# Feed-forward input products by Strassen's scheme, by token, in a two-layer trunk on one core

## What is computed

```python
def swiglu(h, w_in, w_out):                 # h: 512 x 1024, w_in: 1024 x 5632, w_out: 2816 x 1024
    gate, up = jnp.split(h @ w_in, 2, axis=-1)
    return (jax.nn.silu(gate) * up) @ w_out
x = x + 0.5 * swiglu(rmsnorm(x, norm_ffn1[layer]), w_ffn1_in[layer], w_ffn1_out[layer])
```

## Time and profile before

| | us |
|---|---|
| Median of three runs | 2101.12 |
| The profiled execution's own time | 2099.39 |
| Its span, first to last instruction | 2097.6 |
| TensorE busy | 2049.8 |
| VectorE busy | 960.4 |
| ScalarE busy | 592.3 |
| GpSimd busy | 244.6 |
| Granted TensorE clock, mean | 0.99 of full speed |

### The profile page before, as it was taken

One profiled execution on the slowest core, in us unless ns is written; L12 is line 12 of the kernel. 1 busy time (PEld: TensorE's weight loads), 2 busy tenths in 40 slices (PEclk: granted clock), 3 DMA queues, 4 the chain that ended last, 5 costly groups with the idle time before them and its releaser, 6 DMA issues.

```text
span 2097.6 us, 23288 instructions
## 1 busy us (share of the span) xinstructions
PE 2049.8 (98%) x9138; PEld 1674.5 (80%) x9138; DVE 960.4 (46%) x1173; ACT 592.3 (28%) x705; POOL 244.6 (12%) x155
## 2 busy tenths in 40 slices
PE   7999999999999999999999999999988899999997
PEld 5888888777877887888888788888867688888886
DVE  5444434433533444444444444443459754444333
ACT  4222222232222222222222222222256523222210
POOL 3000022110010141000022000002212050000021
PEclk9999999999999999999999999999989999999998
DMA  4222223222212222222223222223221022222221
GB/s 176 100 100 86 77 98 101 102 77 91 80 66 101 81 100 81 100 100 100 69 97 115 89 91 100 100 76 100 91 91 41 21 81 83 97 100 94 83 97 68
DMA packets 30962, 188.73 MB, mean 90 GB/s; under 512 B 3584, under 2 KB 3584, under 8 KB 14656
## 3 DMA queue, kind: packets, MB, share of 16 engines
q1 hardware_dynamic: 30672, 187.25, 25.6%
q0 software_dynamic: 240, 0.79, 0.1%
HBM read 185.92 MB, written 2.10 MB: 90 GB/s over the span
## 4 chain that ended last, share of the span: by engine, by line
PE 94%; DVE 3%; issue 1%; ACT 1%; DMA 0%; POOL 0%; POOLq 0%; DVEq 0%; SPq 0%; ACTq 0%
PE bank L1131 28%; PE bank L1133 28%; PE bank L1132 28%; PE bank L1137 2%; PE bank L1138 2%; PE bank L1139 2%; PE bank L1260 2%; DVE xn_lo L748 1%; PE bank L1250 1%; PE bank L1377 1%; PE bank L1366 1%; DVE w_lo L742 0%; PE bank L1414 0%; PE bank L1423 0%; DVE temp L1080 0%
## 5 line engine op out<-in xcount | busy, mean ns | idle before, releaser
L1131 PE MATMUL bank<-xn_hi,w_hi 128*128 128x512 f32 x1672 | 658.9, 394 | 16.5 <-DVE xn_lo L748 16.3
L1133 PE MATMUL bank<-xn_hi,w_lo 128*128 128x512 f32 x1672 | 652.4, 390 | 0.0
L1132 PE MATMUL bank<-xn_lo,w_hi 128*128 128x512 f32 x1672 | 652.3, 390 | 0.0
L480 ACT ACTIVATE w_hi<-w_raw 128x2048 fp32r<-128x2048 f32 (+2 forms) x195 | 335.7, 1722 | 1011.5 <-PE bank L1133 964.6
L742 DVE TENSOR_TENSOR w_lo<-w_raw,w_hi 128x2048 fp32r<-128x2048 f32 (+2 forms) x191 | 406.1, 2126 | 278.1 <-ACT w_hi L480 277.9
L1131 PEld LDWEIGHTS bank<-xn_hi,w_hi 128*128 128x128 f32 x1672 | 314.2, 188 | 88.9 <-DVE xn_lo L748 12.6
L1133 PEld LDWEIGHTS bank<-xn_hi,w_lo 128*128 128x128 f32 x1672 | 314.4, 188 | 66.8
L1132 PEld LDWEIGHTS bank<-xn_lo,w_hi 128*128 128x128 f32 x1672 | 314.5, 188 | 66.6 <-issue 2.2
L1131 PE MATMUL bank<-gated_hi,w_hi 128*128 128x512 f32 x704 | 273.9, 389 | 0.0
L1132 PE MATMUL bank<-gated_lo,w_hi 128*128 128x512 f32 x704 | 273.9, 389 | 0.0
L1133 PE MATMUL bank<-gated_hi,w_lo 128*128 128x512 f32 x704 | 273.9, 389 | 0.0
(11 more groups left out here) (154 smaller groups left out, 1588.4 us busy)
## 6 DMA issues: line engine op xcount, KB each, us to landing
w_raw<-w_ffn_in SPq DMA_DIRECT2D x87, 1024.0 KB, 4.7
w_raw<-w_ffn_out SPq DMA_DIRECT2D x64, 704.0 KB, 4.0
w_raw<-w_ret_in SPq DMA_DIRECT2D x24, 1024.0 KB, 4.8
w_raw<-w_ret_out SPq DMA_DIRECT2D x8, 1024.0 KB, 4.7
w_raw<-w_dsa SPq DMA_DIRECT2D x8, 1024.0 KB, 4.8
x_res<-x_in SPq DMA_DIRECT2D x4, 512.0 KB, 6.8
out<-x_res SPq DMA_DIRECT2D x8, 256.0 KB, 2.0
w_raw<-w_ffn_in SPq DMA_DIRECT2D x2, 512.0 KB, 6.8
```

The costliest lines, as they stand in the source:

```text
L480: nc.scalar.activation(w_hi[u % 2][:, :size], w_raw[u % 2][:, :size], copy)\
L1131: mm(to, w_hi[slot][:, at:at + width], hi, start=start, stop=False)
L1132: mm(to, w_hi[slot][:, at:at + width], lo, start=False, stop=False)
L1133: return mm(to, w_lo[slot][:, at:at + width], hi, start=False, stop=stop)
```

## The change

The input phase is done over for 20 of the 22 tiles, in five groups of four. With x in quarters (x11: features 0 to 511 of tokens 0 to 255, x12: the other features, x21 and x22 the same of tokens 256 to 511) and the weights of four tiles in quarters (w11 and w21 gate, w12 and w22 up; 512 columns each), a group's eight half-size products become seven (Winograd's form), each of 2 blocks of tokens x 4 feature chunks x 3 matmuls of 512 columns, by token. Four sums S1 to S4 of x quarters are made once in a sublayer, four sums T1 to T4 of weight quarters in every group, in place, all on VectorE. A weight quarter or sum is split in two parts of 1024 elements; four part slots (16 KB with hi and lo) are the ring between the splits and TensorE. The seven products are combined from PSUM on VectorE. The gated tiles come out token-major, so TensorE transposes them (fp32, by the identity, 16 of 128x128 a group) and ScalarE stores them. Tiles 20 and 21 (`REST`) are done plainly, by token, ahead of the groups, in four parts.

Beyond that: 1/rms is a per-token scalar, so the broadcast matmul of an ffn goes; the hi and lo of gated tiles are made at the end of the input phase (the hi copies lie where the weights were); the first two output chunks are done together, tile by tile, in `GATED_ORDER`; output weights have four slots; buffers of the ffn, retention and attention stages overlap, so first loads there wait for `unit_done`; rotary and decay tables load at the start of retention; x and weights are loaded in 1 KB rows (`load_rest`) and 2 KB rows (`load_quad`) in place of 8 KB rows; GpSimd's sums wait for the last transposes; loops of the ffn are written out.

Core of the diff (TensorE first, then VectorE, ScalarE):

```diff
+PRODUCTS = ("x11w11", "S1T1", "S2T2", "x12w21", "S3T3", "S4w22", "x22T4")
+GATED_ORDER = [8, 9, 10, 0, 1, 2, 3, 4, 5, 6, 7, 11, 12, 13, 14, 15, 20, 21, 16, 17, 18, 19]
+        def product_of_parts(to, hi, lo, slot, kk, start, stop):
+            part = slice(kk * P, (kk + 1) * P)
+            mm(to, hi, in_four(part_hi[slot])[:, :, part], start=start, stop=False)
+            mm(to, hi, in_four(part_lo[slot])[:, :, part], start=False, stop=False)
+            return mm(to, lo, in_four(part_hi[slot])[:, :, part], start=False, stop=stop)
...
+                for h in range(REST_PARTS):
+                    pe.wait_ge(part_lo_made, parts0 + h + 1)
+                    for kk in range(2):
+                        k = 2 * h + kk
+                        pe.wait_ge(xn_lo_made, CHUNKS * s + k + 1)
+                        for t in range(BLOCKS):
+                            done = product_of_parts(bank[(6, 7, 2, 3)[t]][:, :], tile(xn_hi, k * BLOCKS + t),
+                                                    tile(xn_lo, k * BLOCKS + t), part_slot(h), kk,
+                                                    k == 0, k == CHUNKS - 1)
+                    done.then_inc(part_used, 1)
+                    if h == (3 if s == 0 else 1):
+                        sum_over_features(norm)
...
+                def group_product(g, i):
+                    name = PRODUCTS[i]
+                    to = {"x11w11": 0, "x12w21": 0, "S2T2": 2, "S3T3": 2, "x22T4": 2, "S1T1": 4, "S4w22": 4}[name]
+                    for half in range(2):
+                        h = part_of(g, i, half)
+                        pe.wait_ge(part_lo_made, parts0 + h + 1)
+                        for kk in range(2):
+                            k = 2 * half + kk
+                            for t in range(2):
+                                hi, lo = left(name, k, t)
+                                done = product_of_parts(bank[to + t][:, :], hi, lo, part_slot(h), kk,
+                                                        k == 0, k == HALF_CHUNKS - 1)
+                        done.then_inc(part_used, 1)
+                def turn(g, half):
+                    from_, made = ((v, gated1_made), (p5, gated2_made))[half]
+                    pe.wait_ge(made, 2 * (GROUPS * f + g + 1))
+                    for n in range(2):
+                        pe.wait_ge(gated_stored, TURNED * f + 4 * g + 2 * half + n + 1)
+                        for m in range(2):
+                            for t in range(2):
+                                done = nc.tensor.transpose(tile(bank[6 + n], 2 * m + t),
+                                                           tile(from_[t], 2 * n + m), identity[:, :])
+                        done.then_inc(gated_turned, 1)
+                for g in range(GROUPS):
+                    count = 2 * (GROUPS * f + g)
+                    if g == 0:
+                        pe.wait_ge(mean_done, stat_count(norm))
+                    else:
+                        pe.wait_ge(gate1_summed, count)
+                    group_product(g, 0)
+                    if g == 0:
+                        turn_rest()
+                    else:
+                        turn(g - 1, 0)
+                    if g > 0:
+                        pe.wait_ge(up1_made, count)
+                    group_product(g, 1)
+                    if g > 0:
+                        turn(g - 1, 1)
+                        pe.wait_ge(gate2_summed, count)
+                    group_product(g, 2)
+                    pe.wait_ge(p1_copied, count + 2)
+                    group_product(g, 3)
+                    pe.wait_ge(u2_made, count + 2)
+                    group_product(g, 4)
+                    pe.wait_ge(p5_copied, count + 2)
+                    group_product(g, 5)
+                    pe.wait_ge(u3_made, count + 2)
+                    group_product(g, 6)
...
+                turn(GROUPS - 1, 0)
+                for half in range(2):
+                    for i in range(HALF_TILES * half, HALF_TILES * (half + 1)):
+                        pe.wait_ge(gated_lo_made, tile0 + i + 1)
+                        for d in range(2):
+                            done = out_product(d, 2 * half + d, i, i == 0, i == FF_TILES - 1)
+                        if i == 3:
+                            turn(GROUPS - 1, 1)
```

```diff
+                make_s1()
+                make_s2()
+                if s > 0:
+                    rest(s, 2)
+                    rest(s, 3)
+                mean_square(("norm", s), D_MODEL)
+                sum_lo(0)
+                make_s4()
+                sum_lo(1)
+                product_lo(0, 0)
+                add_quads(0, 0, 1, 0)
+                dve.wait_ge(r_col_done, stat_count(("norm", s)))
+                for g in range(GROUPS):
+                    end = g == GROUPS - 1
+                    if g == 0:
+                        rest_gated_tiles()
+                        product_lo(g, 1)
+                        sum_lo(3)
+                        make_s3()
+                    else:
+                        sum_gate_2(g - 1)
+                        product_lo(g, 1)
+                        gated_1(g - 1)
+                    add_quads(g, 0, 2, 1)
+                    if g > 0:
+                        gated_2(g - 1)
+                    product_lo(g, 2)
+                    if g == 0:
+                        s3_lo()
+                    add_quads(g, 1, 2, None, 0)
+                    product_lo(g, 3)
+                    make_u2(g)
+                    product_lo(g, 4)
+                    if end:
+                        split_unit(u0)
+                    make_v(g)
+                    add_quads(g, 3, 0, 3, 1)
+                    product_lo(g, 5)
+                    sum_gate_1(g)
+                    make_u3(g)
+                    up_2(g)
+                    product_lo(g, 6)
+                    up_1(g)
+                    if not end:
+                        product_lo(g + 1, 0)
+                        add_quads(g + 1, 0, 1, 0)
+                split_unit(u0 + 1)
+                gated_1(GROUPS - 1)
+                gated_lo_of(slice(0, 3))
+                sum_gate_2(GROUPS - 1)
+                gated_lo_of(slice(3, 5))
+                gated_2(GROUPS - 1)
+                gated_lo_of(slice(5, 11))
```

```diff
+        def split_part(f, h, source, ready=None):
+            if h >= REST_PARTS:
+                act.wait_ge(part_used, PARTS * f + part_before(h) + 1)
+            if ready is not None:
+                act.wait_ge(*ready)
+            nc.scalar.activation(in_four(part_hi[part_slot(h)]), source, copy).then_inc(part_hi_made, 1)
...
+                    product_hi(g, 1)
+                    if g > 0:
+                        gate_2(g - 1)
+                        store_turned(g - 1, 0)
+                    product_hi(g, 2)
+                    copy_product(g, 0, p1, p1_copied)
+                    if g > 0:
+                        store_turned(g - 1, 1)
+                    product_hi(g, 3)
+                    copy_product(g, 1, p5, p5_copied)
+                    product_hi(g, 4)
+                    product_hi(g, 5)
+                    product_hi(g, 6)
+                    gate_1(g)
+                    if not end:
+                        product_hi(g + 1, 0)
```

More of the change, by code:

```diff
@@ L85, in broadcast_count @@
 def broadcast_count(which):
[L87 to L88 removed]
+    return len([w for w in STATS[:stat_count(which)]
+                if w[0] == "head" or w[1] == len(SUBLAYERS) or SUBLAYERS[w[1]] == "ret"])
 def square_ops(which):
@@ new lines, in w_space_free, with part_slot, part_of, part_before @@
+    def w_space_free(engine, u):
+        s = stage_of(u)
+        n = u - FIRST_UNIT[s]
+        if SUBLAYERS[s] != "ffn" and n < 2:
+            engine.wait_ge(unit_done, FIRST_UNIT[s] - 1)
+    def part_slot(h):
+        return (2, 3, 0, 1)[h] if h < REST_PARTS else (h - REST_PARTS) % 4
+    def part_of(g, i, half):
+        return REST_PARTS + 2 * (N_PRODUCTS * g + i) + half
+    def part_before(h):
+        return max(m for m in range(h) if part_slot(m) == part_slot(h))
+    def parts_through(f, g, i):
+        return PARTS * f + part_of(g, i, 1) + 1
@@ new lines, in quad_half, with rest_part, in_four, stat_bank @@
+    def quad_half(n, half):
+        return quad[n][:, :].rearrange("p (t c) -> p t c", t=4)[:, :, 2 * P * half:2 * P * (half + 1)]
+    def rest_part(s, h):
+        return rest_raw[s][:, :].rearrange("p (t c) -> p t c", t=4)[:, :, 2 * P * h:2 * P * (h + 1)]
+    def in_four(t):
+        return t[:, :].rearrange("p (t c) -> p t c", t=4)
+    def stat_bank(which):
+        name, n = which
+        return 0 if name == "norm" and n < len(SUBLAYERS) and SUBLAYERS[n] == "ffn" else STAT_BANK
+    def rest_of(t):
+        return cols(rest_gated, t, 2 * P).rearrange("p (n c) -> p n c", n=2)
@@ L538, in _ @@
-                in_pair(FFN_IN_UNITS // 2 - 1, 0)
-                def out_tile(first, i):
-                    for n in range(2):
```

(45 more changed lines are left out.)

831 lines of the change are left out of this document (589 added, 242 removed).

## The result

The changed kernel takes 2046.33 us (2045.07 to 2047.51) against 2101.69 (2099.67 to 2104.12) of the kernel before, measured beside it: ratio 0.9736, with an interval from 0.9719 to 0.9753. That is 55 us less. The forecast was 2035, in a range of 2022 to 2080. The profiled execution's own time is 2046.45, its span 2044.7.

What follows compares the result with a forecast made beforehand. TensorE, busy 98% of the span, was taken as the bound. Phase savings of 73.5 us, less 3.2, 3.0 and 2.4, plus 1.3, gave 66.2: 2099.4 becomes 2033.2, stated as 2035 us, range 2022 to 2080.

Steps and rivals of the forecast that it cites:

- the floor: Input phase: 212.2 us of matmuls, 9.9 of turns and 0.8 of norm sums make at least 222.9 us.
- The 3.2 us of stalls: Groups: 0.2 us of TensorE stall at each of 16 tight places like gated_1 ahead of the turn.
- The first rival: Groups: VectorE paces them, its operations costing full durations; 24 to 32 us more, 2063; chance 0.24.
- 0.93 us a turn for 0.9: Input phases: each turn of 8 transposes costs TensorE 0.9 us, bounded at 0.8 and 1.2; 11 turns per sublayer.
- The stand-still of 5.4 us: First ffn, after the plain tiles: TensorE idles 5.4 us while VectorE waits for sum_over_features ahead of the first parts.
- 1.7 forecast: First ffn, among the 96 plain matmuls ending at 37.8: 1.7 us added for the lower clock.
- The 1.5 us for "VectorE is behind": First ffn, group 0: 1.5 us more after the stand-still, because VectorE is behind there.
- That fits, with 0.5 us late for the second `rest` part: Phase start: VectorE's some 20 us fit TensorE's 22.6 of plain tiles; 0.5 us late behind retention and attention.
- rival 2: Phase edges: late operands from slow rest rows, squeezed x sums or the ring; 5 us a sublayer, 2055; chance 0.10.
- The prediction's own signs: If right: second to fourth input phases of 223 to 226 us, first output matmul near 245, group distance 40 us.
- The late `rest` parts, 3.0 us: Phase starts: second rest part 0.5 us late behind retention and attention, about 2 in the third ffn; 3.0 in all.
- The 0.6 us a sublayer: Phase end: TensorE waits 0.1 us for tile 0 of the order's fourth place, 0.5 for gated_2; 2.4 over four.

Runs made afterwards that it cites:

- experiment 8: Changed kernel with last group's output split behind its seventh product, part slots turned by two, first-sublayer mean_square between first product's lo and add_quads: 2025.64 us.
- Experiment 5: Changed kernel with one more 1024-wide VectorE operation in 16 groups, placed so that gated_1 comes later: 2067.70 us, ratio 0.9839.
- experiment 6: Changed kernel with one more 1024-wide VectorE operation in 16 groups, ahead of the fourth product's lo and make_u2: 2047.71 us, ratio 0.9746.
- experiment 7: Changed kernel with every transpose of the 40 group turns made twice: 2082.25 us, ratio 0.9909.
- experiment 3: Changed kernel with part slots turned by two and first-sublayer mean_square behind the first product's lo and first weight sum: 2033.39 us, ratio 0.9674.
- experiment 2: Changed kernel with the four part slots handed out turned by two: 2035.97 us, ratio 0.9691.

## Why the prediction was right

**What is bounded by what.** Right. TensorE paces the groups, 39.94 us against 39.9, and input phases have 27.2 us of matmuls less. Matmuls on four runs of 128 columns stand 0.227 apart like all others, so the doubt about the floor (222.9, or 222.0 without the last turn) is settled; experiment 8 comes to 222.6.

**VectorE in the groups.** Right in size and in place: 36.4 us busy for 36.1 forecast, and `gated_1` ends at 170.82 by its line where the turn starts at 170.88. Experiment 5 shows that this place has no slack left (1.25 added, 1.25 lost), experiment 6 that the slack elsewhere is real. The 3.2 us of stalls that I put on the 16 such places did not come. The first rival rested on durations in place of start distances. In rows after, a pair of 1024-wide operations starts 2.27 us before the next, 1.135 each, while one lasts 1.22: inputs ready, the next one does start before the last has ended. The section of the Trainium skill that the prediction set against this ("VectorE: DVE Perf Modes", "The DRAIN you can't avoid") says that the next operation waits until the pipe is empty, but also that one which is not held starts earlier. The prediction left the second half out, and these rows agree with it. By an estimate from them, full durations would have cost 40 operations a group 0.08 us each, 3 us more.

**The turns and the clock.** Right: a group of 39.94 us holds 38.09 of matmuls and two turns, so 0.93 us a turn for 0.9, and eight transposes more cost 0.875 (experiment 7). The clock falls behind no turn, with 8 or with 16 transposes. The Trainium skill says in "TensorE: Matmul & The Clock Gate", "Part 4: PE-mode transpose", that the fast clock does not engage for transposes; windows of mostly matmuls with transposes among them, at 1.00 here, do not bear this out. A long stretch of transposes alone occurs in no run here.

**First ffn.** The stand-still of 5.4 us was forecast at 43.2 and came at 44.03 with 5.46. Missed: what the clock does behind it, though the prediction had a price for that elsewhere. Twelve matmuls at 0.43 cost 2.4 us; twelve more at the very start cost as much, for 1.7 forecast. The 1.5 us for "VectorE is behind" in group 0 did not show as a wait, though waits of that size did once the stand-still was shortened (experiments 3 and 8).

**What failed: the start of group 0.** The step reads "VectorE does the update, ..., some 20 us ... That fits, with 0.5 us late for the second `rest` part". It added up VectorE's work against TensorE's 22.6 us and left out two things outside VectorE: which slot each part goes to and who reads it last, and that ScalarE waits for that slot in order, with `s_hi` behind it. The price was 3.6 us in each later phase (experiment 2), 10.4 us of the run in all. It is rival 2's kind of mechanism ("the ring of four parts handing over late", put at 5 us a sublayer), and belonged into the sum. The prediction's own signs say so too: it wanted later input phases of 223 to 226 us and the first output matmul near 245, and 227.8 and 247.8 came. The late `rest` parts, 3.0 us in the same step, did not occur: at 778.18 and in the plain tiles behind it TensorE did not wait, nor in the other two sublayers.

**End of a phase.** The 0.6 us a sublayer that was forecast, for two waits behind the first output matmul, showed as 0.2: the last turn starts 0.40 us behind the matmul before it (1011.27 to 1011.67), where 0.23 is usual. What cost more stood ahead of it: moving one split gave 1.7 in each phase and 6.3 in the run. The walk began at the last product's end; the split that waits for a load and stands ahead of it on two engines was not costed at all.

**The sum.** Forecast 66.2 us on the profiled execution, measured 52.9. By phase the forecast was short by 2.9, 4.5, 3.0 and 4.5 us in the four input phases, 14.9, and long by 0.3 in each output phase; the stages between make up the small rest. The second phase adds up: ring 3.6 and split 1.7, which the forecast had at nothing, and 0.6 for what experiment 8 keeps above 222.0, less 0.8 of stalls and 0.5 of late parts that did not come, make 4.6. In the third the late parts were put at 2.0, which leaves 3.1. In the first the two stretches at the lower clock and the split bring 4.9 more, and the stalls and the lag in group 0, 2.3, did not come: 2.6 of the 2.9.

That the forecast of 2035 lies within 11 us is therefore in part luck: 7.7 us of stalls, late parts and lag in group 0 that did not come covered a good third of the ring, the split and the clock. Without these terms it would have been 2027, which is what the kernel reached once its lists were put right (experiment 8, 2025.64).

No wait in the traces points to VectorE's pace in the groups or to a DMA transfer as a further cause, save the load behind the last group's split.

## What to carry to other kernels

When work moves to an engine that then is 90% loaded, walk its list against the bottleneck's times: one and the same extra microsecond cost 21 us in one place and next to nothing in another. Walk the buffers as well, for a ring changes hands where two schedules meet, and a wait for a slot holds up all that stands behind it on an in-order engine; turning the ring by two slots, an edit of three lines, was worth 10 us. Before crediting a scheme, make its small reorderings alone in the old kernel: here 7 to 11 of 55 us were theirs.

## What the runs showed of the hardware

A stand-still of 5.46 us behind eight small matmuls was followed by twelve matmuls at TensorE's lower clock; waits of 1.6 us and less at nearly the same place (experiment 3) were not. In the kernel before, one wait of 1.31 us behind short matmuls was followed by 3.4 us at a clock of 0.50 and three equal ones were not, so the length of a wait does not settle it.

GpSimd's sums of squares became faster in the ffn. Groups by form, in the kernel before (count | busy, mean ns):

```profile
L393 POOL TENSOR_TENSOR square_sum<-square_sum,square 128x512 f32<-128x512 f32 x51 | 132.2, 2591 | 4.0
```

and in the changed kernel, for ffn and retention:

```profile
L622 POOL TENSOR_TENSOR square_sum<-square_sum,ffn_square 128x512 f32<-128x512 f32 x31 | 52.9, 1708 | 2.4
...
L622 POOL TENSOR_TENSOR square_sum<-square_sum,ret_square 128x512 f32<-128x512 f32 x8 | 22.5, 2818 | 0.6
```

The same 512-wide addition took 2591 ns in the mean over all sublayers, and 2.55 us in an ffn's output phase (seven in 17.87 us); now it takes 1708 ns in the ffn and 2818 in retention. Buffers have other places now, and VectorE other work beside it; which of these did it was not tried.
